# Expert weights in transfers of 2 MB, two row blocks of a weight each, into five slots of twice the size

## The reference

```python
def expert_choice_ffn(h, p):
    ...
    cap = EC_CAPACITY * n_tok // N_EXPERTS
    aff = jax.nn.softmax((t @ p["router_w"]).astype(jnp.float32), axis=-1)
    gate, idx = lax.top_k(aff.T, cap)
    xs = t[idx]
    hid = jax.nn.silu(jnp.einsum("ecd,edf->ecf", xs, p["exp_w_gate"])) * jnp.einsum("ecd,edf->ecf", xs, p["exp_w_up"])
    out = jnp.einsum("ecf,efd->ecd", hid, p["exp_w_down"]) * gate[..., None].astype(t.dtype)
    y = jnp.zeros_like(t).at[idx.reshape(-1)].add(out.reshape(-1, dm).astype(t.dtype))
```

## Time and profile before

| | before |
|---|---|
| median of 3 runs | 2639.61 us (2637.25 to 2640.37) |
| the profiled execution | 2641.38 us, span 2639.7 us |
| granted TensorE clock, mean | 0.958 |
| TensorE busy | 2330.3 us (88%) |
| VectorE busy | 873.8 us (33%) |
| bytes read | 578.5 MB, 221 GB/s over the span |
| expert weight transfers | 384 of 1024 KB |
| median time from issue to landing, expert weights | 18.2 to 18.9 us by group |

### The profile page before, as it was taken

One profiled execution on the slowest core, in us unless ns is written; L12 is line 12 of the kernel. 1 busy time (PEld: TensorE's weight loads), 2 busy tenths in 40 slices (PEclk: granted clock), 3 DMA queues, 4 the chain that ended last, 5 costly groups with the idle time before them and its releaser, 6 DMA issues. The chain is left out here.

```text
span 2639.7 us, 38211 instructions
## 1 busy us (share of the span) xinstructions
PE 2330.3 (88%) x15976; PEld 1176.1 (45%) x15976; DVE 873.8 (33%) x1821; ACT 399.1 (15%) x814; POOL 157.2 (6%) x181
## 2 busy tenths in 40 slices
PE   6598999989999889889999797989988998998885
PEld 2154444434566556566666455324322432332221
DVE  2161233333445535546544213112211212221113
ACT  1111111221222122122131011001000100000001
POOL 0000111110101101101101010000000000000000
PEclk9699999989999999999999898999999999999997
DMA  9731777763211111011110334999999999999995
GB/s 369 278 80 48 260 253 235 247 219 99 52 40 43 30 37 39 25 46 35 29 44 26 83 96 159 406 413 413 414 414 414 413 413 413 413 407 413 413 413 230
DMA packets 262846, 585.52 MB, mean 222 GB/s; under 512 B 23757, under 2 KB 157991, under 8 KB 241575
## 3 DMA queue, kind: packets, MB, share of 16 engines
q1 hardware_dynamic: 245287, 516.12, 52.3%
q0 software_dynamic: 17408, 67.11, 7.2%
HBM read 578.47 MB, written 4.72 MB: 221 GB/s over the span
## 5 line engine op out<-in xcount | busy, mean ns | idle before, releaser
L1767 PE MATMUL bank<-arena,picked 128*64 128x512 f32 x1248 | 288.8, 606 | 40.0 <-DMA arena<-exp_w_up 37.9
L1052 PE MATMUL bank<-arena,w_rkv 128*128 128x384 f32 x768 | 296.7, 515 | 1.6 <-ACT raw_rkv L1233 1.5
L1924 DVE TENSOR_TENSOR x_sum<-x_sum,bank 128x512 f32<-128x512 f32 x180 | 115.7, 684 | 331.5 <-PE bank L1752 331.5
L1767 PE MATMUL bank<-w_exp,picked 128*64 128x512 f32 x800 | 187.2, 611 | 23.8 <-DMA w_exp<-exp_w_up 22.9
L1767 PEld LDWEIGHTS bank<-arena,picked 128*64 128x64 f32 x1248 | 94.4, 138 | 226.8 <-issue 226.0
L650 PE MATMUL bank<-arena,w_xz 128*128 128x384 f32 x448 | 174.3, 533 | 19.9 <-DMA w_xz<-w_in 19.9
L1052 PEld LDWEIGHTS bank<-arena,w_rkv 128*128 128x128 f32 x768 | 134.6, 192 | 79.3 <-issue 14.0
L1791 PE MATMUL bank<-arena,hid 128*64 128x512 f32 x608 | 138.7, 597 | 10.7 <-issue 6.8
L650 PEld LDWEIGHTS bank<-arena,w_xz 128*128 128x128 f32 x448 | 85.8, 203 | 114.6 <-issue 51.2
L1026 POOL TENSOR_TENSOR WI<-WX,cst 128x384 f32<-128x384 f32 x80 | 86.0, 1079 | 735.0 <-DVE WX L1434 518.9
L1767 PEld LDWEIGHTS bank<-w_exp,picked 128*64 128x64 f32 x800 | 61.2, 139 | 145.3 <-issue 145.3
(11 more groups left out here) (371 smaller groups left out, 2744.5 us busy)
## 6 DMA issues: line engine op xcount, KB each, us to landing
arena<-exp_w_gate SPq DMA_DIRECT2D x78, 1024.0 KB, 18.2
arena<-exp_w_up SPq DMA_DIRECT2D x78, 1024.0 KB, 18.5
arena<-exp_w_down SPq DMA_DIRECT2D x76, 1024.0 KB, 18.7
w_ada<-w_ada POOLq DMA_DIRECT2D x64, 1024.0 KB, 5.5
w_exp<-exp_w_down SPq DMA_DIRECT2D x52, 1024.0 KB, 18.9
w_exp<-exp_w_gate SPq DMA_DIRECT2D x50, 1024.0 KB, 18.2
w_exp<-exp_w_up SPq DMA_DIRECT2D x50, 1024.0 KB, 18.5
w_ada<-w_ada SPq DMA_DIRECT2D x32, 1024.0 KB, 17.9
```

The lines of the kernel that those rows point to most:

```text
L1052: mm = pe.matmul(ps[6][:, 0:T], w[:, m % 3, n % 8], hT[:, n % KC], start=(n % KC == 0), stop=(n % KC == KC - 1))
L1767: mm = pe.matmul(ps[b][COLS[j], :], picked[:, e // PACK % 2, k, at:at + 64], halves[j][:, c * 1024 + b * 512:c * 1024 + (b + 1) * 512], st ...
L1924: V.tensor_tensor(y, y if e else x, ps[6 + i % 2][:], ALU.add).then_inc(S("added"), 1)
```

## The change

The transfers have 2 MB instead of 1 MB. A gate or up transfer holds four blocks of 128 rows (`c=4`), a down transfer two (`c=2`). The ring has five slots of 2 MB in the same memory (three in the arena, two in `w_exp`); an expert has 12 transfers, eight of gate and up and four of down. In `up`, the wait for gate and up stands ahead of every second step kk only, and a slot is given back after its fourth row block (`c == 3`), so after 32 instructions and the scatter between. In `down`, the wait stands ahead of every even f, and a slot is given back after every odd f. The matmuls, their order and all other engines are the same; the other engines' waits on `exp_used` follow through `NS` and `UPS`.

```diff
-    RING, NS = HOME + 4, 24
-    UPS = 16
+    RING, NS = (HOME + 4) // 2, 12
+    UPS = 8
...
-    wide = [I[n].rearrange("l e (q c p) n -> p (l e q) c n", p=P, c=2) for n in ("exp_w_gate", "exp_w_up")]
-    tall = I["exp_w_down"].rearrange("l e (q p) n -> p (l e q) n", p=P)
+    wide = [I[n].rearrange("l e (q c p) n -> p (l e q) c n", p=P, c=4) for n in ("exp_w_gate", "exp_w_up")]
+    tall = I["exp_w_down"].rearrange("l e (q c p) n -> p (l e q) c n", p=P, c=2)
...
-        more = sb(st, "w_exp", [P, RING - HOME, 2048])
-        w = [arena[:, n * 2048:(n + 1) * 2048] for n in range(HOME)] + [more[:, n] for n in range(RING - HOME)]
+        more = sb(st, "w_exp", [P, 2 * RING - HOME, 2048])
+        w = [arena[:, n * 4096:(n + 1) * 4096] for n in range(HOME // 2)] + \
+            [more[:, 2 * n:2 * n + 2].rearrange("p j n -> p (j n)") for n in range(RING - HOME // 2)]
...
-                        dst, src = w[g % RING].rearrange("p (c n) -> p c n", c=2), wide[n % 2][:, e * 8 + n // 2]
+                        dst, src = w[g % RING].rearrange("p (c n) -> p c n", c=4), wide[n % 2][:, e * 4 + n // 2]
                     else:
-                        dst, src = w[g % RING], tall[:, e * 8 + n - UPS]
+                        dst, src = w[g % RING].rearrange("p (c n) -> p c n", c=2), tall[:, e * 4 + n - UPS]
...
                 for kk in range(8):
-                    halves = [arrived(e, 2 * kk + j) for j in range(2)]
-                    for c in range(2):
-                        k = 2 * kk + c
+                    if kk % 2 == 0:
+                        halves = [arrived(e, kk + j) for j in range(2)]
+                    for c in range(2 * (kk % 2), 2 * (kk % 2) + 2):
+                        k = 4 * (kk // 2) + c
...
-                                if (c, b) == (1, 1):
+                                if (c, b) == (3, 1):
                                     mm.then_inc(S("exp_used"), 1)
...
-                    wd = arrived(e, UPS + f)
+                    if f % 2 == 0:
+                        wd = arrived(e, UPS + f // 2)
...
-                    mm.then_inc(S("exp_used"), 1)
+                    if f % 2:
+                        mm.then_inc(S("exp_used"), 1)
```

More of the change, by code:

```diff
@@ L1790, in down @@
                             n = 2 * j + b
-                            mm = pe.matmul(ps[4 + b][COLS[j], :], hid[:, f], wd[:, n * 512:(n + 1) * 512], start=(f == 0), stop=(f == 7))
-                    mm.then_inc(S("exp_used"), 1)
+                            mm = pe.matmul(ps[4 + b][COLS[j], :], hid[:, f], wd[:, f % 2 * 2048 + n * 512:f % 2 * 2048 + (n + 1) * 512], start=(f == 0), stop=(f == 7))
+                    if f % 2:
+                        mm.then_inc(S("exp_used"), 1)
                     if f == 4:
```

## The result

The changed kernel takes 2659.39 us (median of four runs, 2657.54 to 2660.03), the kernel before 2638.43 us beside it (four runs, 2636.26 to 2640.37). The ratio is 1.0079, with a 95% interval of 1.0061 to 1.0096: slower by 21 us. The forecast was 2656.7. (Its gate and up transfers hold four blocks of 128 rows; the two blocks of the title are those of a down transfer.)

The account below looks back on a forecast made before the run. The prediction took the DMA engines, which never rest in the expert stage, as the bound; 3.4 + 12.6 + 2.7 - 1.6 = +17.1 us on 2639.6 gave 2656.7 us, range 2643 to 2667.

Parts of the forecast that it names:

- start: Opening of the expert stage: first slots free after 32 matmuls instead of 16, with DMA engines idle, +3.4 us.
- three gathers: Ahead of experts 3, 7 and 11: first release 7.3 us later, 3.1 slack, so 4.2 us empty queue each, +12.6 us.
- end: After the last landing: TensorE 0.8 us late and two f's left instead of one, +2.7 us.
- 192 transfer ends: 384 transfers become 192; each saved end gives a DMA engine back about 8 ns, -1.6 us in all.
- The likeliest case's own range: Range for the forecast of 2656.7 us: 2648 to 2664, with gathers at 2 to 4.7 us each and ends at 0 to 5.
- Ordinary experts: Experts without a gather ahead: first release at 10.1 us after the first up landing, 3.0 us of margin, nothing lost.
- the rival that wanted 32 slow matmuls: Ordinary experts run dry too: longer idle slows 32 matmuls, not 16, 12 us over twelve experts, 2668.7 us; chance 0.08.
- the 7.3 us: Delay of the first release at each later gather: 2.7 us later at the gather plus 4.7 more after it.
- the 0.8 us late: End of the down phase: TensorE reaches the last down transfer's f's 0.8 us after it lands.
- The faster rival: Each transfer's end costs DMA engines a gap that larger transfers halve; at 150 ns, 2629.5 us; chance 0.09.
- Down weights: Rival: down transfers, with two rows 1 MB apart per partition, fall to 409 GB/s, 8.6 us more, 2665.3 us; chance 0.06.
- Picks stay covered: Rival: the 7.3 us at the later gathers are taken up, only start and end remain, 2644.1 us; chance 0.12.

Follow-up runs that it names:

- coarse_e0: Kernel before, 1 MB transfers, with gate and up of expert 0 alone awaited and freed four row blocks at once: 2640.64 us, ratio 1.0008.
- Coarse_up: Kernel before, 1 MB transfers, with gate and up of all experts awaited and freed four row blocks at once, down unchanged: 2658.07 us, ratio 1.0075.
- coarse: Kernel before, 1 MB transfers and ten slots, but awaiting and freeing four row blocks of gate and up, two of down, at once: 2661.34 us, ratio 1.0080.
- coarse_down: Kernel before, 1 MB transfers, with down weights alone awaited and freed two row blocks at once, gate and up unchanged: 2645.03 us, ratio 1.0018.

## Why the prediction was right

The stage's own time rose by 20.5 us in the profiled pair: the spans differ by 18.6, and the stage's first issue was at 1612.72 against 1614.66. By the terms of the sum:

| term | predicted | in the trace | from |
|---|---|---|---|
| start | +3.4 | +3.3 | landing behind the opening gap less the one ahead of it |
| three gathers | +12.6 | +13.1 | 4.3, 4.4 and 4.4 between landings |
| end | +2.7 | +2.7 | last landing to the end of the span: 37.4 against 34.7 |
| 192 transfer ends | -1.6 | 0 | landings 5.120 and 4.972 us apart (medians of gate and up, of down), 2 x 2.560 and 2 x 2.486 before |
| the rest | 0 | +1.4 | 0.5: the stage's first transfer lands 7.8 us behind its issue, before it was 4.8, and 2.56 for the next; 0.9: net of single steps of 0.2 to 1.4 us in both kernels |

The sum was +17.1. The forecast time is only 2.7 us below the measured one because the kernel before, run beside the changed one, came out 1.2 us below the 2639.6 from which the sum starts; the change itself is 3.9 us larger than forecast. The likeliest case's own range, 2648 to 2664, does not come out of its bounds: with 2 to 4.7 us at each gather and 0 to 5 us for the ends they give 2646.7 to 2659.8, and the measured 2659.4 lies just inside.

*Start.* Right: the first release fell 38.0 us behind the stage's first issue instead of 34.5, and coarse_e0 shows that the ten later experts' deep queue does not give it back.

*Ordinary experts.* Right: no gap in any, though the matmuls behind the long idle were slow as assumed. The first rows of expert 2 in the changed kernel:

```profile
1761.14 1.08 PE L1769 MATMUL bank<-w_exp,picked 128*64 128x512 f32 x1 [5.99 <-DMA arena<-exp_w_up]
...
1763.72 0.64 PE L1769 MATMUL bank<-w_exp,picked 128*64 128x512 f32 x1
```

The granted clock there (windows, third number from the end):

```profile
1760.00:1762.00 2.00, 0.86 (x2) 0.33 (x4) 0.00 (x0) 0.00 (x0) 0.00 (x0) 0.60 1.02 406
1762.00:1764.00 2.00, 2.00 (x8) 0.73 (x6) 0.00 (x0) 0.00 (x0) 0.00 (x0) 0.55 1.04 414
1764.00:1766.00 2.00, 2.00 (x10) 0.47 (x6) 0.00 (x0) 0.00 (x0) 0.00 (x0) 1.00 1.02 406
```

The first matmuls take 1.08 and later ones 0.64 us, and the granted clock is 0.60 and 0.55 in the first two windows, its lower level (1.2 GHz) for part of each, then 1.00 again. The slow stretch is no longer behind 5.99 us of idle than behind 3.28: the first 16 matmuls and the scatter's start behind them are 4.9 us apart here, 5.3 there; the rival that wanted 32 slow matmuls fell with that.

*Gathers.* Right in place, cause and size. One inference inside it was too simple: the 7.3 us were put down as 2.7 for the down grain and 4.7 for the up grain. Coarse_up shows that the up grain brings all of it, because the lateness of the last up pair carries through the down phase.

*End.* The sum was right, its parts were not; that both come to 2.7 us is luck. TensorE's timeline and the scatters that follow it, in the changed kernel and, last two rows, in the kernel before:

```profile
2619.02 5.63 PE L1794 MATMUL bank<-arena,hid 128*64 128x512 f32 x24
2626.04 1.13 PE L1753 MATMUL bank<-outs,G 48*128 48x512 f32 x4 [1.39 <-DVE outs L1947]
2628.54 2.08 PE L1753 MATMUL bank<-outs,G 48*128 48x512 f32 x4 [1.37 <-DVE x_sum L1928]
...
2610.88 1.13 PE L1752 MATMUL bank<-outs,G 48*128 48x512 f32 x4 [1.37 <-DVE x_sum L1924]
2613.38 2.08 PE L1752 MATMUL bank<-outs,G 48*128 48x512 f32 x4 [1.37 <-DVE x_sum L1924]
```

The last transfer landed at 2607.28 + 13.7 = 2621.0, and f = 6 started at once: not the 0.8 us late that was expected, since that landing was itself 1.0 late. So the end has 1.7 us for one more f, and 1.0 because the second scatter already takes 2.08 us. In the kernel before that one took 1.13 and the third 2.08. The granted clock is 0.50 (1.2 GHz) during the second scatter here and 1.00 (2.4 GHz) there:

```profile
2628.00:2630.00 2.00, 1.46 (x4) 0.50 (x4) 0.49 (x1) 1.37 (x4) 0.00 (x0) 0.50 0.00 0
...
2610.00:2612.00 2.00, 1.12 (x4) 0.30 (x4) 0.82 (x2) 1.45 (x4) 0.00 (x0) 1.00 0.00 0
```

*Transfer ends.* The mis-sized term: 1.6 us were expected back, nothing came (coarse against the changed kernel: 1008.7 and 1008.2 us). The faster rival, a gap at each end, fell with it. The Trainium skill (DMA: Bandwidth & Descriptors, Rules for kernel authors) asks for at least 1 MiB in a transfer for the most bandwidth. The trace agrees as far as it goes: 1 MB is enough here, 409 GB/s with either size, and no run had less. The 341 and 425 GB/s that the prediction quotes from the Trainium skill (the same page, Bandwidth, Measured) are for transfers issued from GpSimd; those here are issued from SyncE, so 409 against 341 is no contradiction.

*Down weights.* Two rows 1 MB apart in a partition move at 418 GB/s; that rival fell too. *Picks stay covered* fell with the three dips.

What stays open are the 0.9 us of single steps in the rest.

## What to carry to other kernels

With a ring of fixed size, the size of a slot sets how long the consumer holds memory before any of it comes free; here transfers of the smaller size already ran at the full rate, and the larger slots only took slack away. Reckon that slack at the place where the consumer does something else for longest (here a gather), as the time to landing of the first transfer behind it less the time to landing into an empty queue, and count on less than that where the DMA engines are apart (coarse_down); if it is small, move that work into the consumer's idle times before touching the ring. And look at the opening: the first release sets when the whole stream goes on, so work that the first release does not need belongs behind it.

## What the runs showed of the hardware that was not expected

The issue of a transfer is held back by how much is queued, not by the number of transfers: in the changed kernel the first three issues took 0.37 to 0.51 us, the fourth 3.26 and the fifth 4.79, when some 6 to 7 MB stood queued; with 1 MB transfers the eighth to tenth took 2.30 to 2.71. The bytes flowed meanwhile. And it goes by rows rather than bytes: in the kernel before, the issues at 1728.31 and 1733.48, with eight transfers ahead of them that had not landed, seven of these down weights in rows of 8 KB, took 0.43 and 0.47 us, while the one at 1692.85, with seven ahead, all in rows of 4 KB, took 2.49.

A transfer of 2 MB into an empty queue lands in 7.7 to 7.9 us, 2.6 to 2.8 more than its bytes take; one of 1 MB in 4.9, 2.3 more.

The sixteen DMA engines do not end a transfer together (its semaphore counts sixteen ends): in the kernel before, the last one ended 0.3 us behind the first at the start of the stage, at most 4.5 and at the end 3.7, and the landing is the last one's. The distance grows in single steps of 1.0 to 1.4 us, and it shrinks where the engines in front run empty: from 4.5 to 2.2 us behind the gather ahead of expert 11, where the rate sank to 350 GB/s. The page has 128 packets in its instruction queue, 2.10 MB in all, 16 KB each. The four growing steps (landings at 1673.4, 1925.5, 2157.7 and 2407.3) each come 2.3 to 3.8 us behind the start of such a packet (1670.8, 1921.7, 2155.0 and 2405.0), though most of these packets are followed by no such step. That one of them holds up one engine is likely by these times, but no run here shows it.
